# Local attention steps in another order: parts of the turned weights early on ScalarE and VectorE, sums and parts of the result last

## What is computed

```
logits = einsum('bnqgrd,bnkgd->bngrqk', qb, kb) * (ATTN_HEAD_DIM ** -0.5)
logits = where(valid, logits + bias, -inf)
m = maximum(max(logits), sink)
p = exp(logits - m)
p = p / (sum(p) + exp(sink - m))
out = einsum('bngrqk,bnkgd->bnqgrd', p, vb)
```

## Time and profile before

| | |
|---|---|
| median of 3 runs | 1902.14 us |
| the profiled execution: time | 1904.01 us |
| the profiled execution: span | 1902.3 us |
| TensorE matmul busy, share of the span | 97% |
| VectorE, ScalarE, GpSimd busy, share of the span | 47%, 41%, 72% |
| the steps of the local attention in the trace | about 560 to 730 us |

### The profile page before, as it was taken

The page is one execution under the profiler, slowest core; times in us unless marked ns, Lnnn a source line. Parts: engine busy times, 40 slices in busy tenths (PEclk is TensorE's granted clock), DMA queues, the critical chain, the costliest instruction groups (busy, mean ns, idle before and its releaser), DMA issues.

```text
span 1902.3 us, 26191 instructions
## 1 busy us (share of the span) xinstructions
PE 1851.0 (97%) x9597; PEld 1563.5 (82%) x9597; DVE 894.2 (47%) x1765; ACT 784.8 (41%) x1495; POOL 1363.5 (72%) x1211
## 2 busy tenths in 40 slices
PE   7999999999999989999999999999999999999999
PEld 6888888888877777888888888897679888888887
DVE  6677777762026655345502421727652445203410
ACT  4577777754038893242101210568644522101100
POOL 8766666798844458978988988663434669988985
PEclk9999999999999999999999999999999999999999
DMA  7322222223332222422333333222022222333332
GB/s 219 111 67 67 67 67 67 67 67 110 111 95 62 62 73 89 136 69 93 104 88 106 93 90 109 67 62 67 27 80 95 90 67 89 89 104 95 88 106 71
DMA packets 213613, 165.71 MB, mean 87 GB/s; under 512 B 14478, under 2 KB 209873, under 8 KB 213122
## 3 DMA queue, kind: packets, MB, share of 16 engines
q1 hardware_dynamic: 208134, 149.32, 26.8%
q10 hardware_dynamic: 5372, 14.98, 2.4%
HBM read 161.11 MB, written 7.37 MB: 89 GB/s over the span
## 4 chain that ended last, share of the span: by engine, by line
PE 79%; POOL 6%; ACT 4%; issue 4%; DVE 3%; PEld 3%; PEldq 0%; DMA 0%; ACTq 0%; POOLq 0%; DVEq 0%; SPq 0%
PE bank L401 54%; PE bank L483 9%; POOL w_lo L3226 4%; PEld bank L401 2%; PE bank L451 1%; POOL w_hi L3218 1%; PE bank L427 1%; PE bank L1247 1%; PE bank L1584 1%; PE bank L1193 1%; PE bank L1244 1%; PE bank L1791 1%; PE bank L1608 1%; PE bank L2976 1%; PE bank L1223 1%
## 5 line engine op out<-in xcount | busy, mean ns | idle before, releaser
L3226 POOL TENSOR_TENSOR w_lo<-w_raw,w_hi 128x512 fp32r<-128x512 f32 (+1 forms) x572 | 716.8, 1285 | 207.8 <-ACT w_hi L1431 198.4
L3218 POOL TENSOR_TENSOR w_hi<-w_raw,one 128x512 fp32r<-128x512 f32 (+1 forms) x428 | 441.0, 1061 | 241.1 <-PE bank L401 217.7
L401 PE MATMUL bank<-h_hi,w_hi 128*128 128x512 f32 x952 | 381.3, 401 | 1.1 <-POOL w_lo L3226 0.8
L401 PE MATMUL bank<-h_hi,w_lo 128*128 128x512 f32 x952 | 372.0, 391 | 0.0
L401 PE MATMUL bank<-h_lo,w_hi 128*128 128x512 f32 x952 | 371.0, 390 | 0.0
L401 PE MATMUL bank<-a_hi,w_hi 128*128 128x512 f32 x832 | 326.1, 392 | 1.8 <-POOL w_lo L3226 1.4
L401 PE MATMUL bank<-a_hi,w_lo 128*128 128x512 f32 x832 | 324.0, 389 | 0.0
L401 PE MATMUL bank<-a_lo,w_hi 128*128 128x512 f32 x832 | 323.8, 389 | 0.0
L401 PEld LDWEIGHTS bank<-h_hi,w_lo 128*128 128x128 f32 x952 | 178.6, 188 | 38.9
L401 PEld LDWEIGHTS bank<-h_hi,w_hi 128*128 128x128 f32 x952 | 178.9, 188 | 36.1 <-issue 1.4
L401 PEld LDWEIGHTS bank<-h_lo,w_hi 128*128 128x128 f32 x952 | 179.2, 188 | 33.9
(11 more groups left out here) (502 smaller groups left out, 3033.9 us busy)
## 6 DMA issues: line engine op xcount, KB each, us to landing
w_raw<-in_w_ff SPq DMA_DIRECT2D x32, 1024.0 KB, 5.5
w_raw<-in_w_in SPq DMA_DIRECT2D x31, 1024.0 KB, 5.4
w_raw<-in_w_mlp_in SPq DMA_DIRECT2D x16, 1024.0 KB, 5.4
w_raw<-in_w_mlp_out SPq DMA_DIRECT2D x16, 1024.0 KB, 5.7
w_raw<-in_w_in SPq DMA_DIRECT2D x26, 512.0 KB, 4.4
w_raw<-in_w_ssd_out SPq DMA_DIRECT2D x8, 1024.0 KB, 5.7
bias_rows<-bias_row ACTq DMA_DIRECT2D x1, 4096.0 KB, 15.8
w_raw<-in_w_attn_out SPq DMA_DIRECT2D x4, 1024.0 KB, 6.0
```

What stands on the lines that cost most here:

```text
L401: mm = pe.matmul(bank[:, 0:ntok], a, b[:, koff + k, 0:ntok], start=(k == 0 and n == 0), stop=(k == L.kb - 1 and n == 2))
L3218: pool.tensor_tensor(w_hi[:, slot, part], raw[:, slot, part], one[:].broadcast_to([P, n]), ALU.mult).then_inc(split_hi, 1)
L3226: ins = pool.tensor_tensor(w_lo[:, slot, part], raw[:, slot, part], w_hi[:, slot, part].bitcast(F32), ALU.subtract)
```

## The change

The instructions are the same, and their waits too. On ScalarE the two parts of a step that belong to the finished product (`below`, `out_high`) move behind `high`, `probs` and `normed_weights`; on VectorE `low` moves from the end of the step to the place behind `logits`, ahead of `inverse`, `summed` and `out_low`.

```diff
             for u in range(ALL_UNITS + WEIGH_AT - REP + 3):
                 at_step(hooks, u)
-                if u > WEIGH_AT and u % REP == 1:
-                    below((u - WEIGH_AT) // REP)
-                if u > WEIGH_AT and u % REP == 2:
-                    out_high((u - WEIGH_AT) // REP)
                 if 3 <= u < ALL_UNITS + 3:
                     high(u - 3)
                 if u < ALL_UNITS:
                     probs(u)
                 if 1 <= u < ALL_UNITS + 1:
                     normed_weights(u - 1)
+                if u > WEIGH_AT and u % REP == 1:
+                    below((u - WEIGH_AT) // REP)
+                if u > WEIGH_AT and u % REP == 2:
+                    out_high((u - WEIGH_AT) // REP)
...
                 if u < ALL_UNITS:
                     logits(u)
+                if 3 <= u < ALL_UNITS + 3:
+                    low(u - 3)
                 if 1 <= u < ALL_UNITS + 1:
                     inverse(u - 1)
                 if u > WEIGH_AT and u % REP == 1:
                     summed((u - WEIGH_AT) // REP)
                 if u > WEIGH_AT and u % REP == 2:
                     out_low((u - WEIGH_AT) // REP)
-                if 3 <= u < ALL_UNITS + 3:
-                    low(u - 3)
```

## The result

The changed kernel takes **1924.75 us** (median of four runs, 1923.71 to 1926.62) where the kernel before takes 1902.35 (median of four, 1901.55 to 1904.89): 22.4 us slower. The recorded ratio is 1.0112, with an interval of 1.0098 to 1.0126 (the two medians alone give 1.0118). The forecast was 1921, with 1908 to 1927 as its range. The profiled execution took 1926.62 us, its span is 1924.9, which is 22.6 more than before.

What follows compares the result with a forecast made beforehand. TensorE sets the pace, with 14.0 us of `turn` waiting for `low` in local attention. Added chains 22.1, minus 3.7 for gates, plus 0.6 for the reciprocal, less 0.44 at the end, give 18.6 us: 1921 us, range 1908 to 1927.

Steps and rivals of the forecast that it cites:

- The chain: Local attention, exponential of step s to reduction of s+2: 5.49 us instead of 3.95 in wide cycles, 1.54 us added.
- every duration stays: All instructions: none added or removed, each as long as before; `out_low` on VectorE stays at 0.41 us.
- 14 stretches: Chain growth in 14 local-attention cycles: seven wide at 1.54 us and seven narrow at 1.62 us, 22.1 us in all.
- rest of the cycles: gates: Six cycles whose next hook is a gate: `below` no longer stands before `high`, 0.62 us each, 3.7 us saved.
- rest of the cycles: the reciprocal: Eight cycles with a VectorE hook: the reciprocal now stands between `low` and the hook, 0.08 us each, 0.6 us added.
- up to line 427: At the end of local attention, TensorE's delay first fills the 0.44 us it waits for GpSimd now.
- What was to show it: Local attention: over 30 `turn` waits near 30 us, `probs` and VectorE waiting, stretch about 5.5 us, four steps 11.9 us.
- (a): Rival: `below` is done when VectorE reaches the sums, TensorE's holes vanish, 8 us come back: 1894; 6 in 100.
- (b): Rival: only the hand-over from `below` to the sums binds, `out_high` is hidden, some 7 us slower: 1909; 10 in 100.
- (c): Rival: the earlier `low` and the later `logits` cancel, no difference: 1902; 3 in 100.
- (d): Rival: later hooks free projection banks late, line 401 panels wait, 0.8 us more per cycle: 1932; 6 in 100.
- The rule on an emptied pipeline: VectorE's next operation starts only once the pipeline is empty: three chain pairs cost about 0.09 us more each, 1925.

Runs made afterwards that it cites:

- the half of the change that follows it: VectorE has the new order (`low` behind `logits`), ScalarE keeps the order of the kernel before: 1897.73 us, ratio 0.9971.
- hand-overs a step apart, copies ahead of the exponential: Against the changed kernel, sums and `out_low` run a step behind their copies; `below`, `out_high` directly behind `high` on ScalarE: 1899.15 us, ratio 0.9978.
- ScalarE's half alone: `below` and `out_high` behind the division on ScalarE, VectorE as in the kernel before with `low` last: 1949.69 us, ratio 1.0245.

## Why the prediction was right

The direction, the mechanism and nearly the size came out, by 3.8 us too low. Step by step:

**The chain.** Its eleven links, in the order of the forecast's sum, measure 0.62 (628.25 to 628.87), 0.62 (629.49), 0.63 (630.12), 0.88 (631.00), 0.07 (631.07), 0.65 (631.72), 0.62, 0.50 (632.84), 0.43 (633.27), **0.86** (634.13) and 0.07 (634.20): 5.95 us. Ten of the eleven are within 0.03 of the forecast. The experiments show that these links bind: late `below` and late `out_high` cost 18.1 and 9.4 us and add up to the 27 of both.

**The mis-sized term** is `out_low` at 0.41 us, "every duration stays". In the 14 cycles it took 0.42 to 0.98, in all 4.7 us over 14 times 0.41, and with an input from PSUM 4.6 us came back. The 0.41 holds only where no GpSimd instruction is in the way. With 4.7 us the forecast sum of 18.6 would have been 23.3, against 22.4 measured. Before, GpSimd was idle at 12 of the 14 cycles' `out_low` and within 0.1 us of its burst's end at the other two; after, it was busy at 12. The new order moved `out_low` and GpSimd's bursts into each other. The Trainium skill has this on the page "SBUF — State Buffer", section "SBUF: two separate sides": VectorE's second pair of ports is GpSimd's too, and whichever of a GpSimd instruction that reads SBUF and a VectorE instruction with two inputs in SBUF starts first holds the pair for its whole length. The traces agree: 0.94 us with two inputs in SBUF against 0.42 with one, its end 0.28 us behind that of the GpSimd instruction under way in 70 of 70 cases, and in the 11 near ties GpSimd the one that waited. The one at 743.16, within a burst but only 0.43 us long, started 0.13 us before the end of its GpSimd instruction. I had not weighed this page, since the earlier trace rows made GpSimd look harmless. "Does not pace the stretch" is not "does not touch it".

**The sum over the cycles**, from the starts of the exponentials and reductions in both traces:

| | forecast, us | measured, us |
|---|---|---|
| 14 stretches, without `out_low`'s growth | 22.1 | 22.70 |
| `out_low`'s growth | 0 | 4.66 |
| rest of the cycles: gates | -3.7 | -4.64 |
| rest of the cycles: the reciprocal | +0.6 | +0.35 |
| ahead of the first cycle | 0 | -0.23 |
| up to line 427 | -0.4 | -0.80 |
| behind line 427 | 0 | +0.56 |
| span | 18.6 | 22.60 |

The gates gave back 0.77 us each where `below`'s 0.62 were forecast; why 0.15 more, the rows don't settle. A wide cycle took 12.72 us (from step 25; 10.67 before), not 11.9: 0.46 of that is in the stretch, the rest is that I had put the remainder together from links as 6.45 although it was 6.72 in the trace of before and 6.77 after. The forecast of time rests on differences and did not use it.

**What was to show it** did: over 30 waits of `turn` of near 30 us (44 and 32.6), waits of over 1 us in steps s+2 (1.21), `probs` waiting for `logits` over 0.5 us in two steps of each cycle (1.12 and 1.23 in steps 26 and 27, and 1.16 in step 25 as well), ScalarE's busy time unchanged (133.09 against 132.67). In steps s+3 the wait is 0.99, not some 0.6. Wrong was "0.3 or less" in steps s+1: it is 0.54. `low` comes 0.54 behind the reduction as forecast (628.13 being 627.59 + 0.54), but TensorE is at its place earlier, probably since the ring paces it and it has no backlog.

**The rivals.** (a), faster, missed by 31 us. (Its argument has ScalarE come to `below` 2.5 us behind the reduction. By the forecast's own links the copy starts 1.9 us behind it and ends at 2.5.) The rule cited for it is right about the gap, and the half of the change that follows it gained 5.4 us; what it leaves out is who stands behind the moved work in the same queue. (b), only the first hand-over binding, was priced at 1909. The kernel that has only `below` late took 1915.85, 12.7 above the kernel before where 7 were forecast, so its price was some 6 us low; 3.3 of that are again `out_low`, 0.71 us at 629.07 and 9.01 in the 14 cycles. (c), no difference, fell with the 22.4 us. (d) needs panels of line 401 to wait for banks. From 560 to 752 us the trace after has no wait of TensorE at line 401, so there was none. The rule on an emptied pipeline would have given 1925, which is what was measured, but for another reason: `low` after, 0.55 us long at 631.60, is followed by a reciprocal at 632.07, before its end. The links it would have made longer stayed at 0.07. The section of the Trainium skill that the forecast took the rule from ("VectorE: DVE Perf Modes", "The DRAIN you can't avoid") adds that an instruction which is not held starts earlier; the rows agree with that addition.

## What to carry to other kernels

Two engines with in-order queues that hand work to each other are one chain: walk it link by link, start to start, and ask of every moved instruction who stands behind it in its own queue, and whom the one behind it holds. Work that another engine waits for belongs where its engine would wait anyway (here ahead of the exponential, behind what feeds TensorE); taken from the head of the step to that place, the same 0.6 and 0.4 us of copies gave 7 us, and moved behind the longest work they cost 27. When a move shifts instructions of VectorE with two inputs in SBUF, look at what GpSimd does at the new time.

## What the runs showed of the hardware

A subtraction of 128x256 elements on VectorE with both inputs in SBUF took 0.41 us with GpSimd idle. Beside a GpSimd operation on panels in SBUF it took up to 0.98 us in the changed kernel and up to 1.42 in any (at 628.97, hand-overs a step apart, copies ahead of the exponential). It ended 0.28 us behind the GpSimd instruction that it had found under way, in 70 of 70 cases; in 11 more, where GpSimd's had started only 0.014 to 0.031 us ahead, GpSimd's took 0.28 to 0.30 us longer instead. With one input in PSUM it took 0.42 in all 14 cases, 12 of them beside GpSimd. The reductions beside the same bursts, which read their scores from a bank, kept their 0.60 to 0.62 us.

TensorE's mean granted clock from 573 to 752 us was 1.00 in twelve of the thirteen kernels, where TensorE was busy 146.7 to 174.1 of the 179 us, and 0.89 in the one with ScalarE's half alone, where it was busy 142.5.
